# Interleaving all-token experts with row experts in a two-block transformer kernel

## What is computed

```
h = layer_norm_2(DEEPNORM_ALPHA * h + y, ln_g[layer, 0], ln_b[layer, 0])
y = hier_moe(h, ...)        # 4 groups x 4 experts, hidden width 512
h = layer_norm_2(DEEPNORM_ALPHA * h + y, ln_g[layer, 1], ln_b[layer, 1])

def hier_moe(x, wr_g, br_g, wr_e, br_e, w_gate, w_up, w_down):
    g_logits = xt @ wr_g + br_g;  g_idx = top_k(g_logits, 1)   # one group per token
    top_v, top_i = top_k(e_logits of that group, 2)            # two experts in it
    h = silu(xc @ wg) * (xc @ wu);  h = h * gate of that expert (0 where not chosen)
    return h @ wd
```

## Time and profile before

| quantity | value |
|---|---|
| median of three runs | 2466.53 us (2463.03 to 2473.78) |
| the profiled execution's own time | 2459.22 us |
| its span in the trace | 2457.3 us |
| mean granted TensorE clock | 0.952 of full speed |
| TensorE matmul busy, whole span | 2271.4 us (92%) |
| VectorE busy, whole span | 1512.9 us (62%) |
| ScalarE busy, whole span | 1068.1 us (43%) |
| HBM read | 393.40 MB, mean 161 GB/s |

### The profile page before, as it was taken

How to read it: one execution, slowest core, us unless ns; L and a number is a source line. 1 busy time by engine, 2 the same in 40 slices (tenths; PEclk the granted TensorE clock), 3 DMA queues, 4 the chain that set the end, 5 groups by cost and what they waited for, 6 DMA issues and landing times.

```text
span 2457.3 us, 36662 instructions
## 1 busy us (share of the span) xinstructions
PE 2271.4 (92%) x13900; PEld 1894.5 (77%) x13900; DVE 1512.9 (62%) x2349; ACT 1068.1 (43%) x1514; POOL 234.8 (10%) x225
## 2 busy tenths in 40 slices
PE   7999999999999999899999679999989786999997
PEld 6677567999767756799976469987778476998875
DVE  3846365755384636575534565589985166658997
ACT  1142433343114244234433234467764264447775
POOL 1814000101181400011000000000000000000000
PEclk9999889999999989999999689999999998999999
DMA  4332113455333212356533125589964412458995
GB/s 164 124 118 79 52 61 129 163 181 173 119 125 124 70 52 69 131 176 195 185 125 107 43 80 170 192 294 349 346 248 165 144 44 102 157 197 318 353 348 188
DMA packets 109807, 396.86 MB, mean 161 GB/s; under 512 B 12088, under 2 KB 14144, under 8 KB 109376
## 3 DMA queue, kind: packets, MB, share of 16 engines
q1 hardware_dynamic: 108576, 393.45, 46.2%
q10 hardware_dynamic: 1056, 1.06, 0.2%
HBM read 393.40 MB, written 1.06 MB: 161 GB/s over the span
## 4 chain that ended last, share of the span: by engine, by line
PE 68%; DVE 18%; ACT 6%; DMA 5%; issue 2%; SPq 0%; DVEq 0%; ACTq 0%
PE psum L524 66%; DVE W_LO L1526 6%; DMA ring<-in_weights 4%; ACT W_HI L1157 2%; DVE region L1531 2%; PE psum L532 1%; DVE region L1534 1%; DVE RS L1563 1%; ACT region L1162 1%; DMA SQ<-in_weights 1%; DVE region L1538 1%; DVE SQ L1531 1%; ACT L1166 1%; ACT SQ L1162 1%; ACT L1162 0%
## 5 line engine op out<-in xcount | busy, mean ns | idle before, releaser
L1526 DVE TENSOR_TENSOR W_LO<-ring,W_HI 128x1024 fp32r<-128x1024 f32 x434 | 531.7, 1225 | 228.6 <-ACT W_HI L1157 220.2
L1157 ACT ACTIVATE W_HI<-ring 128x1024 fp32r<-128x1024 f32 x434 | 460.8, 1062 | 360.3 <-PE psum L524 219.2
L524 PE MATMUL psum<-HN,ring 128*128 128x272 f32 (+1 forms) x1600 | 382.4, 400 | 16.0 <-DVE HN L1538 16.0
L524 PEld LDWEIGHTS psum<-HN,ring 128*128 128x128 f32 x1600 | 309.6, 195 | 84.2 <-issue 24.9
L524 PE MATMUL psum<-X_HI,W_HI 128*128 128x256 f32 x800 | 228.6, 286 | 27.5 <-DVE W_LO L1526 25.8
L524 PE MATMUL psum<-X_LO,W_HI 128*128 128x256 f32 x800 | 225.7, 282 | 0.0
L524 PE MATMUL psum<-X_HI,W_LO 128*128 128x256 f32 x800 | 225.3, 282 | 0.0
L1166 ACT ACTIVATE region<-psum 128x272 f32<-128x272 f32 (+9 forms) x227 | 89.5, 394 | 285.4 <-PE psum L524 266.0
L1526 DVE TENSOR_TENSOR W_LO<-SQ,W_HI 128x1024 fp32r<-128x1024 f32 x128 | 156.8, 1225 | 40.9 <-ACT W_HI L1157 37.4
L524 PEld LDWEIGHTS psum<-X_HI,W_HI 128*128 128x128 f32 x800 | 154.3, 193 | 30.2 <-issue 23.9
L524 PE MATMUL psum<-FN_HI,W_HI 128*128 128x272 f32 (+1 forms) x592 | 168.5, 285 | 0.0
(11 more groups left out here) (281 smaller groups left out, 4283.2 us busy)
## 6 DMA issues: line engine op xcount, KB each, us to landing
ring<-in_weights SPq DMA_DIRECT2D x615, 512.0 KB, 4.2
SQ<-in_weights SPq DMA_DIRECT2D x128, 512.0 KB, 5.2
XT<-in_x SPq DMA_DIRECT2D x1, 1088.0 KB, 5.2
CST<-in_consts SPq DMA_DIRECT2D x1, 1082.5 KB, 7.4
SQ<-bias_by_distance ACTq DMA_DIRECT2D x1, 1024.0 KB, 5.5
out<-XT SPq DMA_DIRECT2D x8, 128.0 KB, 1.9
PAR<-in_params SPq DMA_DIRECT2D x1, 572.0 KB, 8.3
bias_by_distance<-MIX ACTq DMA_DIRECT2D x1, 12.0 KB
```

What stands on the lines that cost most here:

```text
L524: ins = nc.tensor.matmul(dst, w, x, start=start, stop=stop, skip_group_check=True)
L1157: lane(nc.scalar.activation(W_HI[:, s % SPLIT, :], ring_slot(n), ACT.Copy), split_hi)
L1526: lane(nc.vector.tensor_tensor(W_LO[:, s % SPLIT, :], ring_slot(n), W_HI[:, s % SPLIT, :].bitcast(F32), ALU.subtract), split_lo)
```

## The change

The expert stage becomes a list of steps of one chunk each, made by `experts_order`. After a lead with gate and up of expert 0 and gate of expert 1, row experts begin at once, and the rest of the all-token work stands in blocks of four chunks between the gate and the up part of a row expert: up 1 behind up 4; gate 2 in expert 5, up 2 in 7, gate 3 in 8, up 3 in 10; down 0 to down 2 in experts 12 to 14, down 3 half in expert 15 and half behind the last row down part. The `hidden` steps (the eight instructions of `wide_hidden`) of experts 2 and 3 stand behind the `rows_turn` that closes expert 7 and 10, that of expert 1 ahead of the `rows_turn` of expert 4. Results of all-token experts get storage of their own until their down part runs (`hidden_parts`); `YB` goes, its contents lie in the gathered rows that are no longer needed; `scatter` 0 and 1 run behind experts 13 and 14.

Besides, six of the eight mean sums run inside `y_out`; `order` transposes half of the tokens, counts, and transposes the other half, with two counting matmuls for five; VectorE makes five splits rather than three before `expert_weights`; and SP reads one offset ahead of the first chunk, the others when their group's first chunk comes.

The diff, cut to what the prediction speaks of:

```diff
+                HL_HI, HL_LO = (sb(f"HL_{p}", 4, 256, dtype=F32R, stack=phase) for p in ("HI", "LO"))
...
+        hidden_parts = [(HE_HI, HE_LO)]
+        hidden_parts += [tuple(t[:, e, :].rearrange("p (j n) -> p j n", j=4) for t in (XK_HI, XK_LO)) for e in range(2)] + [(HL_HI, HL_LO)]
...
+                    if m >= 2:
+                        mean_part(2 * l, m - 2)
...
+            def mean_part(r, k):
+                if k == 0:
+                    take("ln_mean", r)
+                dst, done = banks.tile(("ln_mean", r)), banks.filled(("ln_mean", r))
+                banks.await_read(pe, ("moe", r // 2, "total", k // 2) if r % 2 else ("y_out", r // 2, k))
+                mm(dst[:, :256], ones(128, 128), ht(k), k == 0, k == KT - 1, done if k == KT - 1 else None)
...
+                for k in range(0 if r % 2 else KT - 2, KT):
+                    mean_part(r, k)
...
+                pe.wait_ge(sem("before"), l + 1)
                 dst, done = take("iota", l, bank=3)
                 mm(dst[:, :128], ones(128, 128), BEF[:, :], done=done)
...
+                token_rows(l, 0)
+                pe.wait_ge(sem("group_chosen"), l + 1)
+                dst, done = take("counts", l, bank=2)
+                mm(dst[:, 0:8], ones(128, 128), MS[:, 32:40])
+                mm(dst[:, 8:16], BEF[:, :], MS[:, 32:40], done=done)
+                token_rows(l, 1)
...
+            def wide(l, part, e, c):
+                bank = {"gate": 0 if e < 2 else 4, "up": 6 if e else 2}[part]
+                outs = [again("moe", l, part, e, q) if c else take("moe", l, part, e, q, bank=bank + q) for q in range(2)]
...
+            def wide_down(l, e, c):
+                if e + c == 0:
+                    for q in range(4):
+                        take("moe", l, "total", q, bank=4 + q)
+                w = expert_chunk(l, "down", e, c)
+                pe.wait_ge(sem("hidden"), 2 * (GROUP * l + e) + c // 2 + 1)
+                hi, lo = hidden_parts[e]
...
+            def moe_lead(l):
                 splits.marks["moe", l, "start"] = (len(splits.chunks), state["n"])
-                wide(l, "gate", 0, lambda c: gates_turn(l) if c == 3 else None)
-                wide(l, "up", 0, lambda c: (gates_spread(l) if c == 0 else None, gather(l, c)))
+                for c in range(4):
+                    wide(l, "gate", 0, c)
+                gates_turn(l)
+                for c in range(4):
+                    wide(l, "up", 0, c)
+                    if c == 0:
+                        gates_spread(l)
+                    gather(l, c)
                 slots_turn(l)
-                wide(l, "gate", 1, lambda c: gather(l, 4 + c))
-                total = [take("moe", l, "total", q, bank=4 + q) for q in range(4)]
-                for e in range(1, GROUP):
-                    if e > 1:
-                        wide(l, "gate", e, lambda c: None)
-                    wide_down(l, e - 1, total)
-                    wide(l, "up", e, lambda c: None)
-                for e in range(GROUP, NEXP):
-                    rows(l, "gate", e)
-                    if e % GROUP == 1 and e > 2 * GROUP:
-                        scatter(l, e // GROUP - 2, total)
-                    rows(l, "up", e)
-                    if e == GROUP:
-                        wide_down(l, e - 1, total)
-                    else:
-                        if (e - 1) % GROUP == 0:
-                            part = [take("moe", l, "rows", (e - 1) // GROUP - 1, h, bank=1 + 2 * h) for h in range(2)]
-                        rows_down(l, e - 1, part)
-                    rows_turn(l, e)
-                rows_down(l, NEXP - 1, part)
-                scatter(l, 2, total)
+                for c in range(4):
+                    wide(l, "gate", 1, c)
+                    gather(l, 4 + c)
...
+            def gate_out(l, e):
+                for q in range(2):
+                    act.wait_ge(sem("hidden"), 2 * (GROUP * l + e - 1) + q + 1)
+                    evacuate(("moe", l, "gate", e, q), SGM[:, 2 * q : 2 * q + 2, :], 512, ACT.Silu)
...
+                lane(nc.vector.tensor_copy(MS[:, 40:44], MS[:, 56:60]))
+                tt(MS[:, 44:48], MS[:, 60:64], MS[:, 48:52], ALU.add)
...
+            def wide_hidden(l, e, q):
+                at = slice(2 * q, 2 * q + 2)
+                hi, lo = hidden_parts[e]
+                src = wait_bank("moe", l, "up", e, q)[:, :].rearrange("p (j n) -> p j n", j=2)
+                banks.await_read(dve, ("moe", l, "gate", e, q))
+                free(nc.vector.tensor_tensor(HE[:, at, :], src, SGM[:, at, :], ALU.mult), "moe", l, "up", e, q)
+                tt(HE[:, at, :], HE[:, at, :], bc(GB[:, e : e + 1, :], [128, 2, 256]), ALU.mult)
+                split_tile(hi[:, at, :], lo[:, at, :], HE[:, at, :], sem("hidden"))
...
+            def abreast(l, *step):
+                follow.to(min(splits.marks["step", step[0], l, *step[1:]][0] + SPLIT - 1, splits.first["moe", l, "last"] + 1))
...
-                for i in range(2):
-                    follow.to(first("gate", 0) + 2 + i)
-                    x_tok_low(l, i)
...
+                follow.to(first("gate", 0) + 3)
+                x_tok_low(l, 0)
+                follow.to(first("gate", 0) + 4)
+                x_tok_low(l, 1)
+                follow.to(first("gate", 0) + 5)
...
+            def hidden(l, e, q):
+                abreast(l, "hidden", e, q)
+                wide_hidden(l, e, q)
...
-                    for s in range(4):
-                        group_at[l, s] = sp.value_load(ORD[0:1, s : s + 1], min_val=0, max_val=3 * GROUP_ROWS)
+                if (l, g) not in group_at:
+                    group_at[l, g] = sp.value_load(ORD[0:1, g : g + 1], min_val=0, max_val=3 * GROUP_ROWS)
...
+def experts_order(l):
+    row = lambda part, e: [("rows_down" if part == "down" else "rows", l, *(() if part == "down" else (part,)), e, c) for c in range(4)]
+    wide = lambda part, e: [("wide", l, part, e, c) for c in range(4)]
+    down = lambda e: [("wide_down", l, e, c) for c in range(4)]
+    hidden = lambda e: [("hidden", l, e, q) for q in range(2)]
+    s = [("moe_lead", l)] + row("gate", GROUP) + row("up", GROUP) + wide("up", 1) + hidden(1) + [("rows_turn", l, GROUP)]
+    for e in range(GROUP + 1, NEXP):
+        s += row("gate", e)
+        if e < 3 * GROUP:
+            between = {1: wide("gate", 2), 3: wide("up", 2), 4: wide("gate", 3), 6: wide("up", 3)}.get(e - GROUP, [])
+        else:
+            between = down(e - 3 * GROUP)[: 4 if e < NEXP - 1 else 2]
+        s += between + row("up", e) + row("down", e - 1)
+        s += [("rows_turn", l, e)]
+        for u in (2, 3):
+            if ("wide", l, "up", u, 3) in between:
+                s += hidden(u)
+        if e > 3 * GROUP and e < 3 * GROUP + 3:
+            s += [("scatter", l, e - 3 * GROUP - 1)]
+    return s + row("down", NEXP - 1) + down(3)[2:] + [("scatter", l, 2), ("moe_done", l)]
...
-        s += [("y_out", l), ("layer_norm", 2 * l), ("router", l), ("order", l), ("moe", l)]
+        s += [("y_out", l), ("layer_norm", 2 * l), ("router", l), ("order", l)] + experts_order(l)
```

227 lines of the change are left out of this document (107 added, 120 removed).

## The result

The changed kernel takes 2477.39 us (median, 2469.74 to 2487.2, 20 runs), the kernel before 2471.77 us (2463.03 to 2479.16, 20 runs beside it). The ratio is 1.003 with an interval of 1.0019 to 1.0041: 0.3% slower, which a measurement resolves here and which is less than the 0.5% that the prediction took as its bound. The profiled execution's own time is 2471.89 us, its span 2470.0 us, against 2459.22 and 2457.3. The kernel before was measured anew in each later comparison (medians 2467.79 and 2466.59 us), so times are subtracted only within one comparison.

A forecast was written before the change was run, and what follows sets the result against it. TensorE was taken as nearly full, its waits of 25.4 us (1.0% of the span) capping any gain. Terms of -27.5 and +29.4 us net +1.9 on 2459.2; with the median 7.3 us higher, about 2468 us, range 2452 to 2486.

The forecast's parts named there:

- the case held as likeliest: Whole kernel: the forecast of about 2468 us, its own range 2458 to 2478, chance 0.60.
- (a): Old transition behind up 3: TensorE's 2.8 us wait behind eight VectorE instructions goes from there, gain 5.6 us.
- (b): Mid-stage waits from late transfers and thin VectorE slack: 9.5 of 11.5 us gained, bounds 0 and 11.5.
- (c): Tail, last down part behind its turn: shorter HS_LO waits and no clock fall, gain 3.8 us, bounds 0 and 5.
- (d): Last scatter: its 1.3 us wait for YB_LO goes, gain 2.6 us in both layers.
- (e): Lead: earlier first transfer and small instructions behind the fifth split, gain 6.0 us, bounds 3 and 8.
- (f): Moved pieces of experts 1 to 3, now before row chunks: waits of 3.0, 4.1 and 4.1 us per layer, cost 22.4.
- (g): Clock: four waits of 4.1 us each bring a fall of 1.6 us, cost 6.4 us.
- (h): Mean sums: six lengthen y_out, fewer remain behind its last column, cost 0.6 us.
- B: Moved pieces cost little: each wait stays at 2.8 us or below and the clock holds, 2456 us; chance 0.15.
- C: VectorE becomes the bound between the pieces, mid-stage waits stay and places cost more, 2486 us; chance 0.20.
- D: Row stages: weight-load busy time shows TensorE headroom, 50 us comes free, 2418 us; chance 0.05.

The follow-up runs named there:

- after_again: The changed kernel run once more, unaltered, beside other runs: 2479.37 us, ratio 1.0042 to the kernel before.
- before_lead: The kernel before with only the edits ahead of the first expert (one register load, counting sums between transposes, five splits): 2461.06 us, ratio 0.9975.
- sums_behind: The changed kernel with all eight mean sums behind the output projection again: 29.06 us from projection to variance in layer 0, against 28.61 in the changed kernel.
- spread: The changed kernel with pieces 1 and 2 moved into the next all-token gate blocks and piece 3 halved among row chunks: 2452.18 us, ratio 0.994.
- spread_tail: The kernel with pieces re-placed among all-token gate blocks, plus an all-token down chunk between last turn and last row down part: 2444.69 us, ratio 0.9919.
- warm: The changed kernel with eight unused float32 matmuls on TensorE in each of the four long waits: 2470.77 us, ratio 1.0014.
- halves: The changed kernel with each moved piece in two halves, the second ahead of the next row gate part's last chunk: 2461.03 us, ratio 0.9986.
- one_load: The kernel before with only one register load, not four, ahead of the first transfer: 2465.47 us in one execution, against a median of 2466.59.

## Why the prediction held, step by step

The predicted 2468 us lies 9 us under the measured median; the case held as likeliest, within 0.5% of no change, came out. Step by step, both layers, on the profiled executions:

(a) **Old transition**, -5.6 predicted: gone, as said.

(b) **Mid-stage waits**, -9.5 predicted. Beside pieces and tail, layer 0 has 17.3 - 12.8 - 2.35 = 2.2 us left and layer 1 17.6 - 12.8 - 2.34 = 2.5. The gain is 11.5 - 4.6 = 6.9. The direction is right; I had not seen that the reading of a group's results (1.42 us on VectorE) costs 1 us by itself at two places per layer.

(c) **Tail**, -3.8 predicted. Waits of 2.35 and 2.34 us for 3.12 and 2.60, and the clock 1.00 behind it in this execution: -1.0 - 1.7 = -2.7. In after_again the clock fell behind the tail of layer 1, so the 1.7 us is not a sure gain. The estimate of 1.8 us for turn, `HS_HI` and `HS_LO` was 0.5 short.

(d) **Scatter**, -2.6 predicted: no wait on it is left.

(e) **Lead**, -6.0 predicted. To the gates' transpose it is 35.74 us for 38.31 in layer 0 (-2.6, predicted 2.3) and 33.93 for 37.66 in layer 1 (-3.7, predicted 3.7), and before_lead gave 6.7 by the medians. Not foreseen was that a wait of 2.10 us at the transpose would bring the clock down in layer 0, +1.5.

(f) **Moved pieces**, +22.4 predicted, 2 x 12.8 = +25.6 measured. The first piece was 3.07 for 3.0. For the second and third I took 2.2 us from turn to the end of `HS_LO`, "the least"; the earlier trace rows showed 3.0 with it in plain sight and I put that down to a late VectorE. Here `HS_LO` ends 2.6 us behind the turn's start, since `HS` and four splits stand ahead of it. With 2.6 the prediction's own sum gives 4.5 us, and from matmul to matmul the wait is 4.60; that the weight load's row shows just the upper bound, 4.9 us, is chance. This is the term that was most mis-sized, by 3.2 us, about half by `HS_LO` and the rest by taking a wait on TensorE for a wait of its weight load.

(g) **The clock**, +6.4 predicted for four falls of 1.6 us, +8.8 measured, inside the bounds. All four came, and in two of them the second window too was near the lower level.

(h) **Mean sums**, +0.6 predicted: about +0.5 by the comparison under sums_behind. It lies ahead of the distance in the table.

The sum with the measured terms is -5.6 - 6.9 - 2.7 - 2.6 - 6.3 + 1.5 + 25.6 + 8.8 = +11.8 us. The table of distances gives +14.2, 2.4 us more. They lie in the waits: the terms have 9.5 us more of them, the matmuls' starts 11.9, because most waits read from the weight load are some 0.25 us too long, and the kernel before has 23 of them in the terms where the changed one has 13. The medians put the difference at 5.6 us in one comparison and 11.6 in another (the intervals of the two ratios, 1.0019 to 1.0041 and 1.0026 to 1.0059, overlap); the sum by the profile had been +1.9. The forecast was thus some 4 to 10 us too low in the difference, mostly from (f), (b) and (g), 3.2, 2.6 and 2.4 us. The net is a small difference of two large sums, 24.1 us of gains for 27.5 predicted and 35.9 of costs for 29.4, so that it stayed within 0.5% owes something to luck; that the moved pieces and the clock behind them would eat up the gains is what was foreseen. Of the 9 us by which the median passes 2468, the other 5 lie in the kernel before, whose median was 2466.53 in the three runs that the prediction had and is 2471.77 here.

**The rivals.** B, pieces that cost little: refuted for these places, each wait was over 2.8 us; but spread shows that it was open to the change to have it, by other places. C, VectorE bound between the pieces: refuted, mid-stage waits did not stay at 5 us, and transfers caught up (0.87 of the share with room left). D, by the rule of the Trainium skill (Perfetto Trace Analysis, section Identifying the Most-Contended Engine) that weight-load busy time shows the headroom: refuted. In the row stretch above, the weight load is busy 40.10 of 50 us and would leave 20% free, yet the best kernel here removed most of the waits and came to 0.8% less.

## What to carry to other kernels

When one engine prepares operands for another and is three chunks ahead, as VectorE is here, a burst on it costs (burst + the next operand) minus what the three chunks last on the other engine. At the old transition that gives 5.3 + 1.25 - 4.1 = 2.4 us for a measured 2.8 (2.5 from matmul to matmul), and halving the burst took 2.64 us from each wait. So place bursts where the chunks behind them are the long ones, and note where the burst really runs, which is ahead of the point at which the program marks it. A schedule that evens out the load of all engines gains only the waits there were (25 us here), and one misplaced burst of 5 us, six times, takes it all back. The Trainium skill (Perfetto Trace Analysis, section Optimization Strategy) says that interleaving regimes with different bottlenecks may help; spread and spread_tail bear it out (0.994 and 0.9919, of which the lead alone gives 0.9975), and the changed kernel shows how it fails. Count the clock behind a wait too: it added a third to the price of the pieces (8.8 us to 25.6), and a wait filled with useless matmuls was cheaper than the same wait idle.

## What the runs showed of the chip

How long TensorE waited didn't by itself decide whether its clock fell. Behind the twelve waits of 4.86 us in three executions (the changed kernel twice, and sums_behind) it always fell. Behind 2.97 to 3.07 us at the first piece it held in five of eight cases (four in the changed kernel, one in sums_behind) and fell in three (warm twice, sums_behind once), at the same place of the same instructions. Behind the tail's 2.33 to 2.35 us it fell in four of twelve cases (spread in both layers, halves and after_again in one each) and held in eight. Near 2 us it fell behind 2.10 us (changed kernel, the gates' transpose, 0.50), 2.22 us (halves, third piece, both layers) and 2.02 us (spread_tail, layer 0, 0.57), and it held behind 2.22 us (halves, second piece, both layers), 2.18 and 2.04 us (spread, third piece, both layers) and 2.03 us (spread_tail, layer 1). What the cases that fell have in common is not settled here. A wait of 2 to 3 us is thus to be priced with a chance of 1.5 us more, and one near 5 us with 1.5 to 2.8 us more, as each of the four in the changed kernel cost. It also makes executions of one kernel differ that have the same waits.

The same matmuls can come at two paces at the same granted clock. Windows of 65 us among the all-token experts of layer 0, in the kernel before and at the same place in one_load:

```profile
1530.00:1595.00 65.00, 65.00 (x576) 65.00 (x576) 39.25 (x40) 27.91 (x28) 0.00 (x0) 1.00 0.58 193
1526.00:1591.00 65.00, 65.00 (x555) 65.00 (x554) 38.19 (x39) 26.77 (x28) 0.00 (x0) 1.00 0.56 187
```

TensorE has no gap in either, and the step from matmul to matmul is 0.113 us in one and 0.117 in the other. It cost one_load 3.0 us in this stage. Elsewhere the slower pace held for a few chunks at a time; it cost 0.85 us in both layers together in the changed kernel and 2.2 us in after_again. Nothing in the traces tells what sets it. A difference of 2 or 3 us between two single executions proves nothing for this reason too.

A register load on SP, 0.27 us by its own duration in the earlier trace rows and 0.47 for the first, takes 0.56 us of the path with the two register instructions behind it: the four of the kernel before start 0.55 to 0.57 us apart, but for the longer first. The Trainium skill (DMA: Bandwidth & Descriptors, section Latency and other measured facts) gives about 600 ns as the floor of a `tensor_load`. The step from load to load is near that, but 0.17 us of it are the register instructions' own, and the load's row is 0.27 us; here the path to the first transfer is to be reckoned with the step and not with the row.
